# A 32-byte spacer in the on-chip memory map, between the input tile and the activations, in a two-layer hybrid decoder trunk

## The reference

```python
for l in range(2):
    x = x + 0.5 * swiglu(rms_norm(x, ffn1_norm[l]), w_gate, w_up, w_down)   # 1024 -> 2816 -> 1024
    z = rms_norm(x, mix_norm[l]) @ w_in[l]
    x = x + concat([diff_attention(q, k, v), conformer_conv(zc), short_conv(zs)]) @ w_out[l]
    hq = rms_norm(x, xa_norm[l]) @ xa_wq[l]                                 # 4 heads of 256
    kv = rms_norm(mem, mem_norm[l]) @ xa_wkv[l]                             # 256 memory tokens
    x = x + softmax(hq @ mk.T / 16) @ mv @ xa_wo[l]
    x = x + 0.5 * swiglu(rms_norm(x, ffn2_norm[l]), w_gate, w_up, w_down)
return rms_norm(x, final_norm)
```

## Time and profile before

| what | value |
|---|---|
| median of 3 runs | 1149.58 us (1149.40 to 1149.96) |
| the profiled execution's own time | 1149.58 us |
| its span, from first to last instruction | 1147.8 us |
| granted TensorE clock, mean | 1.00 |
| TensorE busy with matmuls | 1140.2 us, 6180 matmuls |
| VectorE busy | 851.1 us |
| ScalarE busy | 653.4 us |
| GpSimd busy | 21.6 us |
| DMA, mean rate | 184 GB/s |

### The profile page before, as it was taken

The page is one execution under the profiler, slowest core; times in us unless marked ns, Lnnn a source line. Parts: engine busy times, 40 slices in busy tenths (PEclk is TensorE's granted clock), DMA queues, the critical chain, the costliest instruction groups (busy, mean ns, idle before and its releaser), DMA issues.

```text
span 1147.8 us, 15676 instructions
## 1 busy us (share of the span) xinstructions
PE 1140.2 (99%) x6180; PEld 985.8 (86%) x6180; DVE 851.1 (74%) x1164; ACT 653.4 (57%) x937; POOL 21.6 (2%) x63
## 2 busy tenths in 40 slices
PE   9999999999999999999999999999999999999997
PEld 8888888888889888888888888888888888888886
DVE  7767667899967676666786676669998676766756
ACT  6555556547755564545565554565577556645444
POOL 1000000000000000000000000000000000000000
PEclk9999999999999999999999999999999999999999
DMA  8865645644444366555546655544545443656551
GB/s 284 316 207 171 206 157 180 220 148 170 166 167 158 113 224 204 181 190 195 191 152 244 202 183 193 193 162 168 184 147 209 158 147 128 220 175 208 173 191 61
DMA packets 66265, 210.92 MB, mean 184 GB/s; under 512 B 5008, under 2 KB 24208, under 8 KB 61072
## 3 DMA queue, kind: packets, MB, share of 16 engines
q1 hardware_dynamic: 65216, 209.26, 53.6%
q10 hardware_dynamic: 976, 0.66, 0.2%
HBM read 208.85 MB, written 1.05 MB: 183 GB/s over the span
## 4 chain that ended last, share of the span: by engine, by line
PE 95%; DVE 4%; DVEq 1%; issue 0%; ACT 0%
PE G L1663 28%; PE G L1667 15%; PE D L1531 10%; PE D L1532 10%; PE D L1533 10%; PE G L1624 3%; PE D L1624 3%; PE G L1531 3%; PE G L1533 3%; PE G L1532 3%; PE G L1630 2%; DVE w_lo L974 1%; PE D L1630 1%; DVE acc L1181 1%; PE D L1598 1%; DVEq L1183 1%
## 5 line engine op out<-in xcount | busy, mean ns | idle before, releaser
L974 DVE TENSOR_TENSOR w_lo<-w_raw,w_hi 128x2048 fp32r<-128x2048 f32 (+3 forms) x260 | 452.2, 1746 | 54.8 <-ACT w_hi L563 53.8
L563 ACT ACTIVATE w_hi<-w_raw 128x2048 fp32r<-128x2048 f32 (+3 forms) x260 | 381.6, 1476 | 39.5 <-PE D L1533 16.9
L1663 PE MATMUL G<-a,w_hi 128*128 128x512 f32 x1406 | 339.7, 390 | 0.0
L1663 PEld LDWEIGHTS G<-a,w_hi 128*128 128x128 f32 x1406 | 260.8, 188 | 52.7 <-issue 0.9
L1667 PEld LDWEIGHTS G<-a,w_lo 128*128 128x128 f32 x1406 | 184.2, 191 | 9.5
L1667 PE MATMUL G<-a,w_lo 128*128 128x256 f32 x1406 | 187.0, 282 | 0.0
L1078 DVE TENSOR_TENSOR zqk<-G,zqk 128x512 f32<-128x512 f32 x88 | 60.7, 690 | 153.5 <-ACT zqk L642 153.2
L642 ACT ACTIVATE zqk<-G 128x512 f32<-128x512 f32 x88 | 52.4, 595 | 180.8 <-PE G L1667 180.5
L1531 PE MATMUL D<-w_hi,hT_hi 128*128 128x512 f32 x352 | 138.2, 393 | 0.0
L1532 PE MATMUL D<-w_lo,hT_hi 128*128 128x512 f32 x352 | 137.9, 392 | 0.0
L1533 PE MATMUL D<-w_hi,hT_lo 128*128 128x512 f32 x352 | 137.0, 389 | 0.0
(11 more groups left out here) (261 smaller groups left out, 1270.1 us busy)
## 6 DMA issues: line engine op xcount, KB each, us to landing
w_raw<-w_dram SPq DMA_DIRECT2D x120, 1024.0 KB, 5.0
w_raw<-w_dram SPq DMA_DIRECT2D x143, 512.0 KB, 5.4
m_raw<-memT_dram SPq DMA_DIRECT2D x2, 1024.0 KB, 9.4
w_raw<-w_dram SPq DMA_DIRECT2D x6, 256.0 KB, 5.8
w_raw<-w_dram SPq DMA_DIRECT2D x8, 128.0 KB, 4.0
vx<-mem_dram SPq DMA_DIRECT2D x1, 1024.0 KB, 10.7
x<-x_dram SPq DMA_DIRECT2D x2, 256.0 KB, 4.9
gbc<-fin_dram SPq DMA_DIRECT2D x1, 512.0 KB, 7.6
```

Source lines behind the costliest of these rows:

```text
L563: A(w_hi[:, part(i)], w_raw[:, part(i)], ACT.Copy).then_inc(s_hi, 1)
L974: V.tensor_tensor(w_lo[:, part(i)], w_raw[:, part(i)], w_hi[:, part(i)].bitcast(F32), ALU.subtract).then_inc(s_lo, 1)
L1663: M(banks[b], whi[:, at:at + P], both, start=k == 0, stop=False)
```

## The change

One unused tile of 8 float32 per partition (32 bytes) is allocated between `x` and `a`. It is never read or written. Every tile from `a` on begins 32 bytes later; `w_raw`, `w_hi`, `w_lo` and `x` stay. No instruction is added, removed or moved: the engines' programs are the same but for the addresses.

```diff
         w_hi = sb("w_hi", [P, RING], F32R)
         w_lo = sb("w_lo", [P, RING], F32R)
         x = sb("x", [P, TT, D])
+        sb("spacer", [P, 8])
         a = sb("a", [P, KD, 2, T], F32R)
         a_hi, a_lo = a[:, :, 0, :], a[:, :, 1, :]
         m = sb("m", [P, KD, 2, T], F32R)
```

## The result

The changed kernel takes 1164.5 us (median of four runs, 1164.23 to 1164.89) against 1149.54 us before. The ratio is 1.013, with a 95% interval of 1.0118 to 1.0142: 15 us slower. The forecast was 1160.4 us, slower, with a range of 1143 to 1176.

The account below looks back on a forecast made before the run. The prediction took TensorE's end-to-end matmuls to bound the kernel. Its terms -5.5 + 10.3 + 6.0 = +10.8 us on 1149.6 gave 1160.4 us, with a range of 1143 to 1176.

Parts of the forecast that it names:

- no effect: Rival: the trace's differences come from the kinds of neighbouring matmuls, not from addresses; 1149.6 us, chance 0.11.
- the seams: Weights-moving matmuls beside loads of `vx_hi` and `probT` should fall from 397 to about 388 ns, beside `mean_r` rise to 397.
- `kx` products: Sign: `m` stationary, `kx` moving, 256 columns; both move together, so they should keep 117 ns and 283 ns on entry.
- (a): The 1822 matmuls of 256 columns gain 3.0 ns each, from 120.0 to 117: 5.5 us less.
- (b): The 2016 matmuls of 512 columns with weights moving lose 5.1 ns each: 10.3 us more.
- the disturbed five: Five 512-column matmuls right after a 256-column run, 232 ns each; their 5.1 ns excess was the price used in (b).
- (c): The 1726 matmuls of 512 columns with activations moving lose 3.5 ns each, carried over from `kx`: 6.0 us more.
- the 3.67 to 3.70 named as the sign: Sign: 16 matmuls of 512 columns on line 1663 should take 3.67 to 3.70 us instead of 3.63.
- 32 modulo 64 costs, being apart as such does not.: Premise from the matmul beside the `mean_r` load, 320 apart (0 modulo 64): 388 ns, no loss, against 397 at 288 apart.
- settles: Rival: 512-column runs get back into step 32 bytes off too, (b) and (c) are 0; 1141.9 to 1144.1 us, chance 0.22.
- full price: Rival: all 3742 matmuls of 512 columns lose 8 ns, 256-column ones gain nothing; 1179.5 us, chance 0.13.

Follow-up runs that it names:

- `hT` kernel: 32-byte spacer in front of `hT_hi` alone, `a` and `m` left alike with the weights, against the kernel before: 1153.89 against 1149.62 us, ratio 1.0038.
- `am`: 32-byte spacer in front of `a`, filler bringing `hT` back into place, so only `a` and `m` are off, against the kernel before: 1160.89 us, ratio 1.0097.

## Why the prediction was right, point by point

**The direction, and the mechanism.** Right: TensorE bounds everything, nothing else moved, and two reads of one engine at one time cost by the distance of their addresses. The move of everything together (no effect) and the seams in the `hT` kernel (397 to 388 ns, with the same neighbours) show it. The rival "no effect" is out, and the rule of the Trainium skill that was weighed against the mechanism (SBUF — State Buffer, "Who interferes with whom") does not hold for this engine's two reads here: 15 us say otherwise. What inside the memory makes the two reads collide is not shown. The `kx` products, whose distance the change leaves as it was, kept 117 ns (ten steps in 1.17 us) and 282 ns on entry, as forecast.

**(a), the short ones.** Forecast -5.5 us, measured -3.6. The term was oversized: 117 ns was right for after (117.5 on the mean), but before they average 119.5, not 120.0, since each run begins with one of 113, and after the change that first one takes 118.

**(b), long ones with weights moving.** Forecast +10.3 us, measured +9.3, at 4.6 ns instead of 5.1. This is close in part by luck. Out of step they cost 6 to 7 ns more than in step (227.1 to 233.3 in the run of 72), which is more than the 5.1 of the disturbed five; but those that stand behind short ones were out of step before as well, and the twelve of an FFN chunk rose by only 4.1 ns on the mean (229.0 to 233.1).

**(c), long ones with activations moving.** Forecast +6.0 us, measured +9.4. This is the term of the sum that was mis-sized. It was carried over at 3.5 ns from a run of short matmuls, on the argument that a collision costs the same per matmul whatever its length; the long ones pay 5.5 on the mean, and 6.6 in an FFN chunk (226.7 to 233.3), where all sixteen were in step before. So sixteen take 3.73 us and not the 3.67 to 3.70 named as the sign. Why a short one hides part of the price is not shown; that it is held up by its load anyway is only an argument. Had (c) gone by the disturbed five, as (b) did, it would have been 1726 x 5.1 = 8.8 us, and the forecast 1163.2.

**"32 modulo 64 costs, being apart as such does not."** Wrong. It rested on one matmul beside the load of `mean_r`, 320 bytes (64 modulo 256) apart. At such a place 320 apart is indeed free, also beside `probT` and `vx_hi` in the `hT` kernel; yet the spacer of 64 bytes costs 12 us. A single matmul that meets an odd load out of a steady run tells little of what a run of them costs.

**The rival "settles".** It fell, and the `hT` and `am` kernels show why it was half true: like pairs do settle, there within six matmuls, and odd ones do not, not even in the run of 72. **The rival "full price"** fell as well. Its own mark was about 6 ns on the average long matmul, and the average is (9.4 + 9.3) us / 3741 = 5.0 ns; besides, the short ones gained, which it excluded. In an undisturbed run the price comes near to it, 6.6 ns of the 8.

## What to carry to other kernels

When TensorE is the bound and its matmuls run end to end, compare how far apart equal ones start with what their columns need, and look at the addresses of the stationary and the moving operand modulo 256 bytes. Here, in runs of one length, both alike gave 226.7 ns for 512 columns and the other distances tried 230 to 234, so place small tiles of odd length behind the large operands or pad them to 256 bytes (a stray 32 bytes between them is enough to lose 1.3%), and keep runs of matmuls of one length together. Where long and short ones alternate, measure: there the 32 bytes helped. A price read at a seam between two kinds of work is a hint at a mechanism; the price of a steady run has to be read in a run.

## What the runs showed of the hardware

- The distance of the two operands of TensorE counts: 0 and 256 bytes apart give 1149.6 us, 32, 64, 128 and 480 apart 1161 to 1166 us, and 32 bytes on both together nothing (ratio 1.0001).
- It is a matter of step: with like operands, long matmuls that were thrown out of step return from 232 to 227 ns, within five or six behind a run of short ones and within nine behind products with an odd `w_lo`; with operands 32 apart they stay at 233 through a run of 72.
- What counts is the load for the next matmul beside the stream of the present one: at single places among matmuls of 389 ns, 288 apart gave 397, 352 apart 391, and 320 apart 388 ns.
- A short matmul between two long ones takes 116.8 ns on the mean instead of 119.4 in a run, but the long ones take 236.4 instead of 228.0: 353 ns a pair with like operands, against 348 with the spacer.
- Even in step, 512 columns take 226.7 ns where 2.4 GHz gives 213.3. No distance tried brought a long run below that. What the remaining 13.4 ns are stays open.
